# Gated features of two heads turned inside the last read-out, the router by tokens, and products nobody reads in TensorE's waits

## What is computed

```python
hn = hf * lax.rsqrt(jnp.mean(hf * hf, axis=-1, keepdims=True) + EPS)   # per head, 256 features
hn = hn.reshape(B, T, ML_INNER) * ml_norm
readout = jax.nn.sigmoid(z) * (hn + ml_skip * x_c)
merged  = (sigmoid(g_mla) * y_mla + sigmoid(g_ml) * readout) @ w_out
x = x + g1 * merged
aff = jax.nn.softmax(h @ w_router, axis=-1)      # h = modulated norm of x, 16 experts
g, idx = lax.top_k(aff.T, 32)                    # 32 tokens for each expert
y = (silu(xs @ w_e_gate) * (xs @ w_e_up)) @ w_e_down * g
```

## Time and profile before

| what | value |
|---|---|
| median of 3 runs | 1708.28 us |
| the profiled execution | 1701.2 us |
| its span, first to last instruction | 1699.4 us |
| PE busy | 1511.7 us (89%) |
| DVE / ACT / POOL busy | 489.6 / 525.2 / 601.3 us |
| mean granted TensorE clock | 0.968 |
| HBM read | 393.19 MB |

### The profile page before, as it was taken

One profiled execution on the slowest core, in us unless ns is written; L12 is line 12 of the kernel. 1 busy time (PEld: TensorE's weight loads), 2 busy tenths in 40 slices (PEclk: granted clock), 3 DMA queues, 4 the chain that ended last, 5 costly groups with the idle time before them and its releaser, 6 DMA issues.

```text
span 1699.4 us, 17483 instructions
## 1 busy us (share of the span) xinstructions
PE 1511.7 (89%) x7424; PEld 1010.9 (59%) x7424; DVE 489.6 (29%) x803; ACT 525.2 (31%) x683; POOL 601.3 (35%) x167
## 2 busy tenths in 40 slices
PE   5999999999999999999999999989887676676756
PEld 4776678877777658887788886657642131131111
DVE  2222333331222232332244346567410000000001
ACT  5255353433425524434344434254210000000000
POOL 4655187734655517774447671010000000000000
PEclk9999999999999999999999999889898898998898
DMA  6533355598453435569725443000799999999996
GB/s 239 185 124 125 124 176 179 183 334 292 157 178 111 147 125 175 177 198 380 252 91 174 149 138 96 1 15 1 299 405 423 421 421 421 422 421 422 422 422 285
DMA packets 125496, 395.38 MB, mean 233 GB/s; under 512 B 6743, under 2 KB 10644, under 8 KB 101228
## 3 DMA queue, kind: packets, MB, share of 16 engines
q1 hardware_dynamic: 123536, 388.66, 61.6%
q0 software_dynamic: 1456, 4.52, 0.7%
q10 hardware_dynamic: 428, 1.10, 0.2%
HBM read 393.19 MB, written 1.05 MB: 232 GB/s over the span
## 4 chain that ended last, share of the span: by engine, by line
PE 70%; DMA 23%; DVE 2%; ACT 2%; issue 1%; SPq 1%; ACTq 0%; DVEq 0%
PE psum L1960 16%; PE psum L1962 16%; PE psum L1961 16%; DMA ring<-in_w_e_down 6%; DMA arena<-in_w_e_gate 5%; DMA ring<-in_w_e_up 4%; PE psum L1952 4%; PE psum L1056 4%; DMA arena<-in_w_e_down 3%; DMA ring<-in_w_in 2%; DMA hT<-in_w_e_up 2%; DMA arena<-in_w_e_up 2%; PE psum L2191 1%; PE psum L973 1%; PE psum L844 1%
## 5 line engine op out<-in xcount | busy, mean ns | idle before, releaser
L593 POOL TENSOR_TENSOR ring_lo<-ring,ring_hi 128x2048 fp32r<-128x2048 f32 x101 | 467.8, 4636 | 362.2 <-ACT ring_hi L574 362.2
L1960 PE MATMUL psum<-ring_hi,hT_lo 128*128 128x512 f32 (+2 forms) x912 | 366.5, 402 | 16.1 <-DVE hT_lo L2209 10.6
L1962 PE MATMUL psum<-ring_hi,hT_hi 128*128 128x512 f32 (+2 forms) x912 | 356.8, 391 | 0.0
L1961 PE MATMUL psum<-ring_lo,hT_hi 128*128 128x512 f32 (+2 forms) x912 | 354.5, 389 | 0.0
L574 ACT ACTIVATE ring_hi<-ring 128x2048 fp32r<-128x2048 f32 x116 | 222.1, 1915 | 385.4 <-DMA ring<-in_w_in 123.0
L1056 PE MATMUL psum<-arena 128*32 128x512 f32 x740 | 169.6, 678 | 57.0 <-DMA arena<-in_w_e_gate 21.2
L1960 PEld LDWEIGHTS psum<-ring_hi,hT_lo 128*128 128x128 f32 x912 | 172.4, 189 | 58.6 <-issue 12.2
L1056 PE MATMUL psum<-ring,arena 128*32 128x512 f32 x708 | 156.6, 664 | 56.0 <-DMA ring<-in_w_e_down 19.9
L1962 PEld LDWEIGHTS psum<-ring_hi,hT_hi 128*128 128x128 f32 x912 | 172.1, 189 | 38.2
L1961 PEld LDWEIGHTS psum<-ring_lo,hT_hi 128*128 128x128 f32 x912 | 173.0, 190 | 33.9 <-issue 0.5
L1056 PEld LDWEIGHTS psum<-arena 128*32 128x32 f32 x740 | 36.0, 121 | 161.7 <-issue 55.9
(11 more groups left out here) (390 smaller groups left out, 1644.3 us busy)
## 6 DMA issues: line engine op xcount, KB each, us to landing
ring<-in_w_in SPq DMA_DIRECT2D x60, 1024.0 KB, 5.2
ring<-in_w_up SPq DMA_DIRECT2D x32, 1024.0 KB, 5.6
ring<-in_w_down SPq DMA_DIRECT2D x32, 1024.0 KB, 5.8
arena<-in_w_e_gate SPq DMA_DIRECT2D x31, 1024.0 KB, 26.7
arena<-in_w_e_up SPq DMA_DIRECT2D x31, 1024.0 KB, 27.0
ring<-in_w_e_gate SPq DMA_DIRECT2D x30, 1024.0 KB, 26.7
ring<-in_w_e_up SPq DMA_DIRECT2D x29, 1024.0 KB, 27.0
ring<-in_w_e_down SPq DMA_DIRECT2D x29, 1024.0 KB, 27.0
```

The lines of the kernel that those rows point to most:

```text
L593: eng.tensor_tensor(slot_lo(u), slot(u), slot_hi(u).bitcast(F32), ALU.subtract).then_inc(done, 1)
L1960: pe.matmul(dst, lo(k0 + k), w_hi, start=start and k == 0, stop=False)
L1961: pe.matmul(dst, hi(k0 + k), w_lo, start=False, stop=False)
L1962: last = pe.matmul(dst, hi(k0 + k), w_hi, start=False, stop=stop and k == nk - 1)
```

## The change

1. Gates' map: `gates_map(0)` is dealt out over rounds 5 to 8 (two blocks a round), `gates_map(1)` over rounds 14 and 15, and the other steps move to rounds 1, 3, 10 and 12.
2. `keep_busy(bank, count)`: `count` f32 products of the identity with itself (128x128x128) into a PSUM bank that nobody reads. It stands at nine places in TensorE's program: before the first wait of each layer of the first block (11), before the `t_sb` wait of the last attention round of each layer (6), before the second block's attention (4), in the two waits for the mLSTM scans (14 and 5), before the first weights of the mLSTM (3), and in the two waits of the router (11 and 9).
3. Head pairs: VectorE takes the means of heads 0 and 1 inside `weights(3)`, gates them before the read-out of head 2 and sums them after it. ScalarE loads the root's table right after its last decays. TensorE turns these four eighths between the two halves (`t` = 0, 1) of head 3's numerators. Their low part goes to a place of its own, `gatedT_lo`. Heads 2 and 3 are gated together later, and `turn_gated(1, 3)` stands between the two token halves of `out_unit(1, 0)`.
4. Router by tokens: the last two units of `w_out` are run as (t 0, n 0), (t 0, n 1), (t 1, n 0), (t 1, n 1), and token half 0 is added, turned and copied meanwhile. The logits are 8 products with 16 columns for each token half, tokens on the partitions; the strips and their sum go. ScalarE loads the exponential's table ahead and scales x after the softmax instead of before it. The first MAX8 and MATCH_REPLACE read PSUM, and the copy at L1501 goes.

```diff
-MAP_ROUNDS = (2, 4, 6, 8, 10, 12)
+MAPS = {1: (0, 0, KC), 3: (1, 0, KC), 5: (2, 0, 2), 6: (2, 2, 4), 7: (2, 4, 6), 8: (2, 6, KC), 10: (3, 0, KC), 12: (4, 0, KC),
+        14: (5, 0, 4), 15: (5, 4, KC)}
...
+            def keep_busy(bank, count):
+                for _ in range(count):
+                    pe.matmul(psum[:, bank, 0:P], ident, ident, start=True, stop=True)
...
                 for u, (n, kh) in enumerate(((0, 0), (1, 0), (0, 1), (1, 1))):
+                    if u == 0:
+                        keep_busy(7, 11)
                     pe.wait_ge(turn_lo, l * 18 + 4 * (kh + 1))
...
+                        if j == NJ:
+                            keep_busy(2 * ((NJ - 1) % 2), 6)
                         pe.wait_ge(t_sb, l * NJ + j)
...
             pe.wait_ge(qt_a, 4)
+            keep_busy(2, 4)
             pe.wait_ge(qt_v, 4)
...
+            pe.wait_ge(gr_v, 3)
+            keep_busy(6, 14)
             pe.wait_ge(gr_v, 9)
...
+            pe.wait_ge(vt_a, 2)
+            keep_busy(3, 5)
             pe.wait_ge(gr_v, 12)
...
                     if h:
                         pe.wait_ge(h_v, 8 * h - 2 + 2 * t)
+                    if h == MH - 1 and t == 1:
+                        pe.wait_ge(mix_v, 8)
+                        turn_gated(0, 0)
...
+            pe.wait_ge(h_v, 8 * MH)
+            out_unit(1, 0, gated_rest)
+            router_bias()
             pe.wait_ge(turn_lo, 18 * DEPTH + 2)
...
+            for t, n in ((0, 0), (0, 1), (1, 0), (1, 1)):
+                u = U_OUT + 2 + n
+                if t == 0:
+                    unit_ready(u)
+                if t and n:
+                    pe.wait_ge(x2_v, 4)
+                    pe.wait_ge(rt_v, 2)
+                    turn_token(0, 0)
+                last = split_product(DB[1 + n][:, t, :], tokens(hT_hi, t), tokens(hT_lo, t), UC, u, start=False, stop=True)
+                last.then_inc(slots_free if t else o2_half, 1)
+
+            pe.wait_ge(turn_a, TURN_A + 10)
+            logits(0, 0)
+            logits(0, 1)
+            pe.wait_ge(x2_v, 8)
+            turn_token(1, 3)
+            pe.wait_ge(turn_a, TURN_A + 11)
+            logits(1, 0)
+            pe.wait_ge(turn_v, TURN_V + 10)
+            logits(1, 1).then_inc(lg_full, 1)
+            keep_busy(2, 11)
+            pe.wait_ge(rt_v, 8)
...
             spread(2, 2)
+            keep_busy(6, 9)
+            pe.wait_ge(top_v, 11)
...
             def weights(h):
                 low_out(h)
+                if h == MH - 1:
+                    head_means(slice(0, 4), 4)
                 dve.wait_ge(raw_full, 2 * h + 2)
...
+                if h == MH - 2:
+                    head_gates(0, 5, 2)
                 if h == MH - 1:
-                    head_out(0, 3, 0, 6)
+                    head_sums(0, 6)
+                    dve.wait_ge(turn_a, TURN_A + 9)
+                    low_gated(0, flat[0])
                 dve.wait_ge(num_full, h + 1)
...
                 if h == MH - 1:
+                    act.activation(root_soon, amp1[:, 0, 0:1], ACT.Sqrt).then_inc(at_sb, 1)
+                    act.wait_ge(mix_v, 1)
+                    act.activation(hst[:, 2, 0:4], hst[:, 1, 0:4], ACT.Sqrt).then_inc(hn_a, 1)
                     act.wait_ge(gb_full, 1)
```

More of the change, by code:

```diff
@@ L425, in build @@
         aff = piece(612, TT, NE)
-        root_ahead, table_ahead = piece(692, 1), piece(693, 1)
+        root_ahead, table_ahead, exp_ahead, root_soon = [piece(692 + i, 1) for i in range(4)]
         rst = piece(644, 4, TT)
@@ L804, in turn_block, with gates_map @@
                 last.then_inc(map_full, 1)
-            def gates_map(i):
+            def gates_map(i, c0, c1):
                 pe.wait_ge(rows_in, 32)
-                for c in range(KC):
+                for c in range(c0, c1):
                     if i == 0:
@@ L952, in spread, with turn_gated @@
                 last.then_inc(gb_full, 1)
+            def turn_gated(half, db):
+                for k in range(4):
+                    for t in range(TT):
+                        c = 4 * half + k
+                        last = pe.transpose(flat[db][:, k * T + t * P:k * T + (t + 1) * P], gated[:, t, c * P:(c + 1) * P], ident)
+                last.then_inc(turn_full, 1)
             for h in range(MH):
@@ L975, in tensor_block2, with out_unit @@
                 last.then_inc(num_full, 1)
[L977 to L984, removed]
+            def out_unit(n, kh, between=None):
                 u = U_OUT + 2 * kh + n
@@ L987, in out_unit @@
                 for t in range(TT):
-                    last = split_product(DB[1 + n][:, t, :], tokens(hT_hi, t), tokens(hT_lo, t), UC * kh, u, start=kh == 0, stop=kh == 1)
+                    if t == 1 and between:
+                        between()
+                    last = split_product(DB[1 + n][:, t, :], tokens(hT_hi, t), tokens((gatedT_lo, hT_lo)[kh], t), UC * kh, u, start=kh == 0, stop=kh == 1)
                     if n == 1 and kh == 1 and t == 0:
@@ L1021, in tensor_block2 @@
[L1021 to L1028, removed]
-                    last = pe.matmul(psum[32 * j:32 * j + 32, 0, 0:T], wr[:, k, :], hT[:, k, :], start=half == 0, stop=half == 1)
-            last.then_inc(lg_full, 1)
-            pe.wait_ge(rt_v, 3)
@@ L1032, in tensor_block2, with turn_token @@
-            for t in range(TT):
-                last = pe.matmul(psum[:, 1, t * NE:(t + 1) * NE], part_sums[:, t * P:(t + 1) * P], const("sum16"), start=True, stop=True)
-            last.then_inc(lg_full, 1)
-            pe.wait_ge(rt_v, 9)
+            def turn_token(t, db):
+                for half in range(2):
+                    for k in range(4 * half, 4 * half + 4):
+                        last = pe.transpose(flat[db][:, k * P:(k + 1) * P], eighths(x[:, t, :], k), ident)
+                    last.then_inc(turn_full, 1)
@@ new lines, in logits @@
+            def logits(t, half):
+                for k in range(4 * half, 4 * half + 4):
+                    last = pe.matmul(psum[:, t, 0:NE], hT[:, k, t * P:(t + 1) * P], wr[:, k, 0:NE], start=k == 0, stop=k == KC - 1)
+                return last
+            for t, n in ((0, 0), (0, 1), (1, 0), (1, 1)):
[8 more added lines that the diff above has]
+                last.then_inc(slots_free if t else o2_half, 1)
@@ L1379, in weights, with head_means, head_gates @@
                                              op0=ALU.mult, op1=ALU.mult).then_inc(w_v, 1)
[L1381 to L1383 removed]
+            def head_means(heads, ready):
                 dve.wait_ge(hn_a, ready)
                 dve.tensor_scalar(hst[:, 1, heads], hst[:, 0, heads], 1.0 / MD, EPS, ALU.mult, ALU.add).then_inc(mix_v, 1)
[L1386 removed]
+            def head_gates(h0, ready, mv):
+                heads = slice(TT * h0, TT * h0 + 4)
+                dve.wait_ge(hn_a, ready)
                 dve.reciprocal(hst[:, 3, heads], hst[:, 2, heads]).then_inc(mix_v, 1)
[L1388 removed]
+                dve.wait_ge(mix_v, mv)
                 dve.wait_ge(zg_sb, 4)
[L1390 removed]
+                for h in (h0, h0 + 1):
                     for t in range(TT):
```

155 lines of the change are left out of this document (71 added, 84 removed).

## The result

| | before | after |
|---|---|---|
| median of timed runs | 1706.84 us (1702.53 to 1709.88, 9 runs) | 1696.35 us (1693.25 to 1699.62, 9 runs) |
| profiled execution | 1701.2 us | 1697.94 us |
| its span | 1699.4 us | 1696.2 us |
| mean granted TensorE clock | 0.968 | 0.967 |

The ratio of the runs is 0.9944, 95% interval [0.993, 0.9957]: 9.6 us faster, between 7.3 and 11.9. So a term can be read from this pair, but the sum can't.

What follows compares the result with a forecast made beforehand. Bound: the end of `out_unit(0, 0)`, plus the expert weight stream at 422 GB/s, plus its hole. Terms: 5.0 + 1.7 - 2.7 + 0.4 + 6.9 + 1.7 = 13.0 off the median 1708.28 gave 1695 us, range 1687 to 1703.

Steps and rivals of the forecast that it cites:

- (c): Six unread products in each layer's last attention round: no wait covers them, 1.3 us onto the path twice, -2.7 us.
- (e): Head 3 to `w_out`: copy and low part run beside the second numerators, `out_unit(0, 0)` starts earlier at full clock, +6.9 us.
- (a): Gates' map dealt out over attention rounds: the low clock around the 32 narrow instructions goes, +5.0 us.
- (b): Eleven unread products at the start fit the 7.33 us wait; first dense products run at full clock, +1.7 us.
- (d): Unread products around the mLSTM scans: all covered by waits, raw scores at full clock, only 0.4 us arrives.
- (f): Router by tokens: experts begin 8.1 us earlier, first products at full clock, the weight stream's hole closes, +1.7 us.
- The rule weighed against it: Clock monitor's window runs freely, meeting the kernel at another phase each run; without the map's 5.0 the sum is 8.
- R4: Rival: timed runs lose clock at more waits and unread products take it back, 13 + 4, 1691 us; chance 0.09.
- R2: Rival: handover to `w_out` not shortened, gates and `mix_v` wait late; gain 8.7 in all, 1699.6 us; chance 0.09.
- R3: Rival: unread products in attention rounds and router cost more than they keep, hole reopens, 1712 us; chance 0.06.
- the prediction's spare of 1.8: Expert stage: first products free places at 1234.4, the 17 loads are used up at 1237.2, hole closes with 1.8 to spare.
- R1: Rival: clock falls elsewhere, the map's loss an accident or still tripped by spread work; gain 7.1, 1701 us; chance 0.18.

## Why the prediction was right, and where not

Sign and time held: 1696.35 against 1695, range 1687 to 1703. That the two are so near is in part luck. The forecast gain of 13.0 lies outside what was measured, 9.6 (7.3 to 11.9), and the median it was taken from, 1708.28, was 1.4 above that of nine runs. In the profiles only (c) and (e), and less closely (a), came out at their size; (b), (d) and (f) fell short of the forecast by 6.4 us together, and 3.3 us more were lost in round 8. The steps:

- **(a) Map, +5.0: right for the kernel before.** Alone it is worth 4.9 in timed runs, and both profiles of the kernel before have the fall. The rule weighed against it, by which the 5.0 need not be in the timed runs, did not decide here: the one-piece map fell in all four profiles of kernels without unread products ahead of that attention. In the changed kernel the term isn't seen on its own: two pairs with and without it are level (0.9944 and 0.9941; 0.9933 and 0.9933), within about 4 us each. The profiles offer one reason, that the four products ahead of the attention may hold the clock as well (65.03 with the products and the map in one piece), but that is one execution.
- **(b) Start, +1.7: 0.5 here.** I had the wait and the cost of the eleven right and took the clock to last through what they leave idle. They leave 3.7 us, not 2.4, because they ran at 0.16 us an instruction on the mean, part of them at full clock. Of the eight profiles with products at the start, one (without the last rounds' six) kept full pace throughout; in the seven others the clock was low for part of the dense products, with 18 as with 11. What I missed about layer 1: products there do help. Without them (six profiles) the clock fell in the first dense products of layer 1 in three; with them (eight) in none. R4's premise was right in that.
- **(c) Last round, -2.7: confirmed in the rows**, 1.33 a layer. The runs price it at about 6 in the changed kernel (2.6 to 9.7 from both intervals) and at no more than 1.0 in the kernel before. Why they differ is open.
- **(d) Scans, +0.4: wrong sign, -1.15.** The step "so 0.4 arrives" looked at head 0 only. TensorE, done 2 us sooner, next waited for the same weights ahead of head 1's raw scores, 2.78 us with three products of cover, and lost the clock there. I had not asked what is late next. That holds for all four profiles with head 0 at full clock and three products of cover (2.78 us each time); in two others with the same products head 0 itself was at low clock, and the stretch took 39.4, 0.2 more than before the change.
- **(e) Handover, +6.9: 7.3**, and 42.63 to 42.66 in all profiles that have it. VectorE's read-out of head 2 began 3.9 us after the start of head 3's weights, where I had 4.2, and each link kept its old length. With the turning moved back, 4.2 of it are gone, so that placement is its main part. R2 did not happen.
- **(f) Router, +1.7: failed, -1.9.** The step that broke is "eleven unread products end 0.4 too late". The second logits' clock had already fallen (3.13 us against the first's 1.85), so the eleven took 4.79 instead of 2.4, outlasted the softmax by 2.4 us, and the experts began 40.5 us after the first load. That is R3's place, and more than its price there, because a second step broke with it: "the first expert products take 3.6 at full clock". They took 5.40. In the five profiles with the eleven in place these took 4.3 to 5.1 us, and the hole was 1.7 to 3.6; without them, in one execution with both steps as worked out (37.5, 3.64), there was none. Both steps count: with no unread products at all the experts began at 37.2 and 37.8, but their first products took 6.0 and 5.4, and holes of 1.1 and 0.8 were left.

  What sets the hole is when the 18th load goes out. Seventeen loads of 1.05 MB at 422 GB/s last 42.2 us, and the 18th followed the first by 43.9 before (hole 1.7), 45.9 after (3.6) and 41.2 without the eleven (none). By this the prediction's spare of 1.8 was too wide as well: places come free when the first expert products end, 1231.3 + 3.6 = 1234.9, not 1234.4, and the stream lasts until 1193.6 + 42.2 = 1235.8, which leaves 0.9. In the medians the eleven aren't visible (0.9943 without, 0.9944 with).

R1, "the clock falls elsewhere", was no rival to the forecast but went on beside it: 3.3 us in the profiled execution at two waits of 1.8 us that both kernels have. I listed it as what would replace (a), and gave its loss no term of its own.

Where do the 9.6 us of the median come from? Handover and router alone, with nothing against the clock, measure 11.4, [8.7, 14.2]. So these two carry the gain; the map and the unread products together add nothing to them that can be seen. The products in the last rounds cost about as much (some 6, at least 2.6) as all the others keep (4.1): the best versions, at 0.9896 to 0.9908, are those without the former.

**Open:** why the last rounds' products are dearer in the changed kernel than in the old one, whether dealing out the map is worth anything beside the unread products, and why handover and router measure 11.4 where their rows give about 8. The medians of 4 to 12 runs that differ by where the clock fell resolve none of them.

## What to carry to other kernels

A filler (products that nobody reads) in front of a wait is free only if the wait is there in the profile and longer than the filler *at low clock*, also in the executions in which TensorE comes late to it; where the row shows no idle time, it is plain added work. When a wait is shortened, look for the next instruction that waits for the same producer before booking the gain. And where two profiles of one kernel differ by which waits lose the clock, price such terms by runs of one part alone, not by one pair of traces; a handover that was a serial chain (root, gate, turn, copy, low part) is the sturdier gain, since it came back to 0.03 us in all nine profiles that have it.

## What the hardware showed beyond that

- A fall of the clock among dense products costs 1.4 to 2.7 us: six to thirteen of them go 0.43 instead of 0.23 apart, and then the pace is back. At the one-piece map it cost more, 3.2 to 4.8. It can begin at once after a wait (round 8), or six products later (the start).
- The wait in round 8 of layer 0 stood in twelve profiles, and four of them lost the clock behind it; in layer 1 it was five of twelve. The two executions with six unread products in front of it kept the clock in both layers. With the same 1.86 us, the kernel with head pairs and router only lost it and the one without the last rounds' products did not. The wait's length alone does not tell.
- The record of the granted clock can be silent at the start. In the profile before, it says 1.00 for 20 to 30 us (below, the number before the last two), while the dense products stand 0.43 apart until 23.5. Start-to-start distances are the surer sign there.

```profile
20.00:30.00 10.00, 10.00 (x42) 8.08 (x42) 1.00 (x3) 3.79 (x6) 6.26 (x2) 1.00 0.31 103
```

- An execution from the fast end of its kernel is a poor base: both profiled executions of the unchanged kernel before (1701.2 and 1701.05) lie below the medians of the timed runs (1703.74 to 1706.84), so a sum from it starts low; adding its difference to the median, as the prediction did, was what kept the forecast in place.
